# Layer 1's attention: results normalised and turned per unit, weights and token tiles split ahead inside the unit loop

## The reference, cut to what matters

```python
def rms_norm(x, g):
    xf = x.astype(jnp.float32)
    y = xf * lax.rsqrt(jnp.mean(xf * xf, axis=-1, keepdims=True) + EPS)
    return (y * g.astype(jnp.float32)).astype(x.dtype)

# blocked_diff_attention, for every block of 128 queries
s = jnp.einsum('bqphd,bsphd->bphqs', qblk, k, preferred_element_type=jnp.float32) * scale
pr = jax.nn.softmax(s, axis=-1)
w = (pr[:, 0] - lam * pr[:, 1]).astype(v.dtype)
return jnp.einsum('bhqs,bshe->bqhe', w, v)

# diff_mixer, latent tokens
q, k, v = jnp.split(h @ p['w_in'], 3, axis=-1)
q = rms_norm(q.reshape(B, L, 2, C_HEADS, HEAD_DIM), p['q_gain'])
k = rms_norm(k.reshape(B, L, 2, C_HEADS, HEAD_DIM), p['k_gain'])
...
o = blocked_diff_attention(q, kk, vv, lam)
o = rms_norm(o, p['subln']) * (1.0 - p['lam_init'])
return o.reshape(B, L, C_HEADS * 2 * HEAD_DIM) @ p['w_out'], state
```

## Time and profile before

| | us |
|---|---|
| median of 3 runs | 3526.24 (3525.89 to 3528.17) |
| the profiled execution, its own time | 3528.04 |
| its span in the trace | 3525.4 |
| layer 1's attention in it | about 862 (1686 to 2548) |
| PE busy over the span | 3219.6 (91%) |
| DVE busy | 2253.0 (64%) |
| ACT busy | 1852.7 (53%) |

### The profile page before, as it was taken

One profiled execution on the slowest core, in us unless ns is written; L12 is line 12 of the kernel. 1 busy time (PEld: TensorE's weight loads), 2 busy tenths in 40 slices (PEclk: granted clock), 3 DMA queues, 4 the chain that ended last, 5 costly groups with the idle time before them and its releaser, 6 DMA issues. The chain is left out here.

```text
span 3525.4 us, 54805 instructions
## 1 busy us (share of the span) xinstructions
PE 3219.6 (91%) x19994; PEld 2440.7 (69%) x19994; DVE 2253.0 (64%) x2853; ACT 1852.7 (53%) x2549; POOL 559.1 (16%) x319
## 2 busy tenths in 40 slices
PE   6988989997999999997898998989997899999997
PEld 3447777784667667675687887878885567767665
DVE  3557666644666666665686785867746566666665
ACT  2444647522565666664365473654722556666663
POOL 1001010000322333221101101010000233322220
PEclk9989999996999999998899999999997999999998
DMA  7230000228888888885010100100035588888883
GB/s 242 83 104 21 1 21 1 73 102 319 310 304 291 289 301 288 292 292 159 21 40 7 40 7 2 40 7 22 29 116 226 204 299 296 289 291 293 286 303 115
DMA packets 218313, 566.37 MB, mean 161 GB/s; under 512 B 37845, under 2 KB 75418, under 8 KB 217882
## 3 DMA queue, kind: packets, MB, share of 16 engines
q1 hardware_dynamic: 207760, 530.26, 41.9%
q0 software_dynamic: 9472, 33.57, 4.0%
q10 hardware_dynamic: 906, 0.23, 0.0%
HBM read 525.05 MB, written 38.94 MB: 160 GB/s over the span
## 5 line engine op out<-in xcount | busy, mean ns | idle before, releaser
L2342 DVE TENSOR_TENSOR moe_lo<-moe_raw,moeg_hi 128x2048 fp32r<-128x2048 f32 x384 | 884.6, 2339 | 319.8 <-PE psum L2162 154.9
L2244 ACT CAST moeg_hi<-moe_raw 128x2048 fp32r<-128x2048 f32 x384 | 728.9, 1911 | 426.2 <-PE psum L2180 298.0
L933 PE MATMUL psum<-attn_w_hi,attn_hs 128*128 128x256 f32 (+2 forms) x1440 | 382.8, 350 | 54.5 <-DVE attn_w_lo L1281 27.9
L1397 DVE TENSOR_REDUCE attn_neg_max<-psum 128x1 f32<-128x1280 f32 (+1 forms) x216 | 292.5, 1356 | 79.9 <-PE psum L1038 77.7
L933 PEld LDWEIGHTS psum<-attn_w_hi,attn_hs 128*128 128x128 f32 x1440 | 261.1, 195 | 87.3 <-DVE attn_hs L1275 41.7
L1197 ACT ACTIVATE attn_e<-psum,attn_neg_max 128x1280 f32<-128x1280 f32 (+1 forms) x216 | 265.1, 1227 | 79.3 <-DVE attn_neg_max L1397 61.0
L1038 PE MATMUL psum<-attn_ks,attn_qst 128*128 128x512 f32 (+2 forms) x1200 | 283.0, 369 | 16.3 <-ACT attn_qst L1135 6.5
L1135 ACT COPY attn_pt<-psum 128x512 f32<-128x512 f32 (+2 forms) x400 | 192.7, 508 | 153.4 <-PE psum L1051 139.4
L2180 PE MATMUL psum<-moeg_hi,moeh_x_hi 128*128 128x512 f32 x960 | 265.3, 398 | 4.8 <-issue 4.8
L2180 PE MATMUL psum<-moe_lo,moeh_x_hi 128*128 128x512 f32 x960 | 262.5, 395 | 0.0
L2180 PE MATMUL psum<-moeg_hi,moeh_x_lo 128*128 128x512 f32 x960 | 261.1, 393 | 0.0
(11 more groups left out here) (293 smaller groups left out, 5296.4 us busy)
## 6 DMA issues: line engine op xcount, KB each, us to landing
moe_raw<-in_l_w_gate SPq DMA_DIRECT2D x256, 512.0 KB, 3.9
moe_raw<-in_l_w_up SPq DMA_DIRECT2D x256, 512.0 KB, 5.1
moe_raw<-in_l_w_down SPq DMA_DIRECT2D x128, 1024.0 KB, 6.2
ada_w<-in_l_ada_w SPq DMA_DIRECT2D x32, 1024.0 KB, 14.3
lru_ada<-in_l_ada_w SPq DMA_DIRECT2D x16, 1024.0 KB, 7.4
out_w<-in_l_w_out SPq DMA_DIRECT2D x16, 512.0 KB, 5.5
h_rows<-mix_xs SPq DMA_DIRECT2D x16, 512.0 KB, 2.6
attnw_w<-in_l_w_in SPq DMA_DIRECT2D x16, 512.0 KB, 6.7
```

Of the source, the lines that this page charges most:

```text
L933: last = pe.matmul(out, hs[t % 2][:, part, k, :], right, start=(k == 0 and n == 0), stop=(k == KB - 1 and n == 2))
L1397: dve.tensor_reduce(neg_max[:, n:n + 1], m.psum[:, score_at(n):score_at(n) + hi - lo], AX.X, ALU.max, negate=True).then_inc(s["maxed"], 1)
L2244: act.copy(mm.hi[slot % 4][:, :, :], mm.raw[slot][:, :, :]).then_inc(s["hi_ready"], 1)
L2342: dve.tensor_tensor(mm.lo[slot][:, :, :], mm.raw[slot][:, :, :], mm.hi[slot % 4][:, :, :].bitcast(F32), ALU.subtract).then_inc(s["lo_ready ...
```

## The change

It touches `attention` for layer 1 (layer 0's order and sizes stay as they are):

- The results live in five small tiles (`OUT_TILES`) of 128 by 128 in turn, laid over the split keys `khl`, instead of one big `o`. DVE waits at the start of a group until the last results were turned before it writes the keys there.
- POOL makes mean and power of every unit by itself (two instructions of one column, 18 times per group). ACT multiplies the unit's result by it (`normalise`) at the end of the step in which it was squared.
- PE turns the result of unit `u - 3` into the third quarter of the bank in which part 1 of unit `u`'s probabilities stands; ACT copies it to `cat` with the gain (`read_out`) ahead of that part. So 13 results (units 0 to 12) are turned in the loop, and five are left for `turn_out`, in two banks.
- Where `o` was, only `hs[1]` lies (`hs_space`). ACT casts tile 1 of the next group at the end of a group, ahead of the last two `normalise`; in the first group, ahead of the loop.
- ACT and DVE split token tile 0 of the next group at step 12, and the weights at steps 15 to 19, in the order 2, 0, 4, 1, 7, 3, 5, 6, as the probability tiles beneath come free. PE takes tile 0's blocks in that order.
- `norm_mean` and `norm_out` are gone from DVE.

```diff
-    o = put("o", [P, NT, 4 * HD])
+    put("hs_space", [P, NT, 4 * HD])
+    OUT_TILES, OUT_LAG = 5, 3
...
+    khl_at = put.pos[0]
...
-    TURNS = turns_k + 2 * NT + 3 * (units - per_tile) + per_tile + (0, 6)[l]
+    TURNS = turns_k + 2 * NT + 3 * (units - per_tile) + per_tile + (0, 2)[l]
...
+    if l == 1:
+        o = [m.tensor(f"attn1_o{i}", [P, dv], F32, khl_at + i * dv * 4) for i in range(OUT_TILES)]
+    TOKENS = -1
+    ahead_at = [{27 + i: [i - 1] for i in range(KB + 1)},
+                {12: [TOKENS], 15: [2], 16: [0, 4], 17: [1, 7], 18: [3], 19: [5, 6]}][l]
+    w_order = [k for u in sorted(ahead_at) for k in ahead_at[u] if k != TOKENS]
...
@@ program, end of a step @@
-            if l == 0 and not last and units - AHEAD <= u < units:
-                make["ahead"](u - (units - AHEAD))
+            if not last:
+                for piece in ahead_at.get(u, ()):
+                    make["ahead"](piece)
...
+    osum, orstd = ratio[:, 2 * NT:4 * NT], red[:, nz:nz + 2 * NT]
+    out_with = lambda u: u - OUT_LAG if l == 1 and u >= OUT_LAG and u // per_tile < LT else None
+    last_outs = [u for u in range(units) if u > units - per_tile - 1 - OUT_LAG]
+    out_blocks = [[u for u in last_outs if u % 2 == p] for p in range(2)]
@@ gpsimd @@
-                    for i, (lo, hi) in enumerate(NORM_PARTS):
-                        wait_value(m, pool, s["o_mean"], j * 2 + (i + 1))
...
+                    for u in range(units):
+                        wait_value(m, pool, s["o_squared"], j * units + (u + 1))
+                        pool.tensor_scalar(osum[:, u:u + 1], osum[:, u:u + 1], 1.0 / dv, EPS, ALU.mult, ALU.add)
+                        pool.drain()
+                        pool.tensor_tensor(orstd[:, u:u + 1], osum[:, u:u + 1], m.neg_half[:, 0:1], ALU.pow
+                                           ).then_inc(s["o_rstd"], 1)
@@ tensor @@
-                for k in range(KB):
+                for i, k in enumerate(w_order if t == 0 else range(KB)):
                     if t == 0 and lo == 0:
-                        pe.wait_ge(s["w_split"], j * KB + (k + 1))
+                        pe.wait_ge(s["w_split"], j * KB + (i + 1))
...
+                        if part == 1 and out_with(u) is not None:
+                            pe.wait_ge(s["o_normed"], j * units + (out_with(u) + 1))
+                            last = pe.transpose(m.psum[:, at + 2 * P:at + 3 * P], o[out_with(u) % OUT_TILES][:, :], m.ident[:, :])
                         last.then_inc(s["turned"], 1)
...
                 def turn_out():
...
+                    pe.wait_ge(s["o_normed"], j * units + units)
+                    for block in out_blocks:
+                        at = next_turn()
+                        for i, u in enumerate(block):
+                            last = pe.transpose(m.psum[:, at + i * P:at + (i + 1) * P], o[u % OUT_TILES][:, :], m.ident[:, :])
+                        last.then_inc(s["turned"], 1)
@@ scalar @@
                 def project(t):
-                    split_tokens(j, t + 1)
+                    if l == 0 or t >= 1:
+                        split_tokens(j, t + 1)
...
+                        if part == 1 and out_with(u) is not None:
+                            read_out(out_with(u))
...
                         square_out(u - 2)
+                    if l == 1 and part == 1 and u >= 2:
+                        normalise(u - 2)
...
+                def read_out(u):
+
+                    act.wait_ge(s["turned"], j * TURNS + (turn[0] + 1))
+                    at = turn_bank(used[0]) + 2 * P
+                    out = cat[:, ds(j * 2 + u % 2, 1), (u // 2) * P:(u // 2 + 1) * P].rearrange("p o t -> p (o t)")
+                    act.activation(out, m.psum[:, at:at + P], ACT.Copy, scale=m.subln[:, 0:1])
+
+                def normalise(u):
+                    act.wait_ge(s["o_rstd"], j * units + (u + 1))
+                    act.activation(o[u % OUT_TILES][:, :], o[u % OUT_TILES][:, :], ACT.Copy, scale=orstd[:, u:u + 1]
+                                   ).then_inc(s["o_normed"], 1)
...
-                def ahead(i):
-                    if i == 0:
+                def ahead(piece):
+                    if piece == TOKENS:
                         split_tokens(j + 1, 0)
-                    else:
-                        split_weights(j + 1, [i - 1])
+                        return
+                    values_done = {7: units - 2, 5: units - 1, 6: units} if l == 1 else {}
+                    if piece in values_done:
+                        act.wait_ge(s["pv_done"], j * units + values_done[piece])
+                    split_weight(j + 1, piece)
...
                 if l == 1:
+                    for u in (units - 2, units - 1):
+                        square_out(u)
                     if not last_group:
-                        split_tokens(j + 1, 0)
-                        split_weights(j + 1, EARLY_W)
-                    square_out(units - 2)
-                    square_out(units - 1)
-                    if not last_group:
-                        act.wait_ge(s["pv_done"], j * nvalues + nvalues)
-                        split_weights(j + 1, LATE_W)
+                        split_tokens(j + 1, 1)
+                    for u in (units - 2, units - 1):
+                        normalise(u)
                     turn_out()
@@ vector @@
                     dve.wait_ge(s["cache_loaded"], j * (32 * PT_TILES) + 32 * PT_TILES)
+                    if l == 1:
+                        dve.wait_ge(s["turned"], j * TURNS)
...
+                    if not last_group:
+                        for piece in ahead_at.get(u, ()):
+                            if piece == TOKENS:
+                                split_tokens(j + 1, 0)
+                            else:
+                                split_weights(j + 1, [piece])
                 dve.drain()
-                if l == 1:
-                    if not last_group:
-                        split_tokens(j + 1, 0)
-                        split_weights(j + 1, EARLY_W)
-                    norm_mean(1)
-                    if not last_group:
-                        split_weights(j + 1, LATE_W)
-                    norm_out(1)
-                    dve.drain()
```

More of the change, by code:

```diff
@@ L1466, in group @@
                         maxima(u + 1, 1)
-                    if l == 1 and u == units - 1:
-                        norm_mean(0)
-                    if l == 1 and u == units + 1:
-                        norm_out(0)
                     if l == 1 and u % 2 == 0 and u // 2 + 2 < NT:
```

68 lines of the change are left out of this document (18 added, 50 removed).

## The result

The changed kernel takes 3493.62 us (median of 4 runs, 3490.60 to 3494.95), the kernel before 3527.11 (3525.89 to 3528.17): a ratio of 0.9904, 95% interval 0.9887 to 0.9921. The forecast was 3493.

A forecast was written before the change was run, and what follows sets the result against it. PE was taken as the bound, standing still at group borders and hardly stopping in the units. Borders and end -46.5 - 3.0, units and step 12 +10.6 + 6.2, sum -32.7 us: forecast 3493, range 3477 to 3515.

The forecast's parts named there:

- the late last values: End of a group: weight casts and subtractions make unit 17's probabilities be read about 0.4 us later, charged at each border.
- The borders: Between groups: 114.6 us for three borders fall to 23.5, 23.5 and 21.1, together 68.1, a gain of 46.5.
- PE's branch: Ahead of tile 1 at the first two borders: PE's return to the loop's start, formerly hidden, taken as 2.4 us each.
- the margin of 0.9 for block 6: Border, tile 0: the last weight block is subtracted about 4 us behind the last values, and PE asks 4.9 behind.
- The pair of steps: In the units: a pair pays 0.25 for ACT's normalisation and 0.13 for PE's transpose, 0.38; 10.6 us in all.
- Rival B: In the units: ACT's additions are paid in most steps, needing waits and address registers; 17 less gain, 3510 us; chance 0.15.
- Step 12: Token tile 0's split there makes DVE's next maximum start 2.05 us late; three groups cost 6.2 us.
- The end of the stage: From the last values to the last copy: 8.5 us come to 5 to 6, a gain of 3.
- POOL's chain of 0.9 to 1.9: Per unit: POOL's mean and power with hand-overs, called covered by 2.1 us and another 1.1 of ACT's spare.
- The rule weighed: Port shared by DVE and POOL: whichever starts first blocks the other; trace agrees for POOL as loser, not for DVE.
- C: In 56 steps DVE loses the port to POOL, up to 0.85 us per unit, 48 in all: 3541 us; chance 0.03.
- D: In 56 steps POOL is blocked behind DVE and ACT waits: +67, net +34 us, 3560 us; chance 0.04.

The follow-up runs named there:

- e4: The changed kernel with token tile 0 and all weights split behind step 19 instead of ahead: 3498.06 us, ratio 0.9916.
- e8: The changed kernel with the normalisation one step later (six result tensors, not five) and DVE's token tile 0 subtraction at the end of step 14: 3474.48 us.
- e3: The kernel before with only token tile 0 and the weights split ahead, at steps 12 and 15 to 19; results turned at the border: 3515.19 us.
- e6: The changed kernel with token tile 1 of the next group split behind the turned copies again, as before: 3505.41 us, ratio 0.9944.
- e2: The changed kernel with ACT's normalisation one step later and a sixth result tensor in place of five: 3479.96 us, ratio 0.9864.
- e1: The changed kernel with DVE's subtraction for token tile 0 at the end of step 14 instead of step 12: 3489.39 us, ratio 0.9896.
- e5: The changed kernel with one more four-column POOL power, its result unused, ahead of each unit's mean: 3514.06 us, ratio 0.9956.

## Why the prediction was right, and where it wasn't

The mechanism was right: the two waits at each border went, and the units and step 12 paid for it about as forecast. One term failed, the late last values, and the time came so near because errors cancelled.

- *The borders.* 23.5, 23.5 and 21.1 were forecast, 68.1 together; 22.6, 23.7 and 21.7 came, 68.0. Inside, the terms differ and cancel. PE's branch is 1.39 and 1.52, not 2.4, but in e4 and e8 it was 2.07 and 1.72. Tile 0 is 8.9 at the first border, not 8.5: the margin of 0.9 for block 6 was nearer to nothing, and the wait didn't return in full. At the other two it is 10.2, at a clock of 0.64 for its first 4.7 us, which no term had. That the sum of the borders came out to 0.1 us is luck. e3, e4 and e6 show that all three parts are needed for it.
- *The pair of steps.* +0.38 forecast, +0.39 measured, and e2 splits it as forecast (0.27 for ACT's 0.25, and 0.12 left for PE's 0.13). Per group it came to 2.0 to 2.2, not the 2.65 of seven full pairs. The prediction read 0.79 and 0.43 as the idle stretches of all even steps; the kernel before has 0.43 in nearly every pair, and 0.79 once in a looped group, at step 12. The pair that ends there took 13.24 already, so it grew by only 0.03. The rest of ACT's work was hidden as argued: ACT's wait ahead of the turned tiles on odd steps fell from 1.11 to 0.65. Rival B's registers do exist, 0.23 of issue ahead of each looped `read_out` (9.1 us in all), and vanish in ACT's waits for the maximum and for the turned tiles.
- *Step 12.* 2.05 forecast, 1.9 measured (15.16 less 13.27), and e1 and e8 showed its cause. Without a normalisation between exponential and cast (e3) it is 1.4. The third group lost 1.4 more to the clock behind it, which the sum didn't have.
- *The end of the stage.* 3.0 forecast, 2.6 measured.
- *The last values 0.4 late: mis-sized.* They are 1.4 late in each of three groups. The step that failed is the one that let the weight casts alone set this term and called POOL's chain of 0.9 to 1.9 "covered". The chain is 1.5, inside those bounds, and covered in the wide steps, where `read_out`, a copy and a 1.33 us exponential stand before the normalisation. In the last narrow steps there is nothing to cover it, and ACT waits 1.44. The cover was looked up for one kind of step and used for all. But the wait costs only together with the casts. From PE's start on step 14's probabilities to the end of the last values, in the first group, it took 17.61 before, 18.00 with the weights ahead alone (e3: the 0.4 of the forecast), 17.88 with the turning alone (e4), 19.25 with both, and 18.32 with both in e2's order. So 0.93 of the lateness belongs to neither part: ACT waits for POOL, then makes two weight casts of 1.55 together, and only then copies the last probabilities. In the fourth group, which has no casts, ACT waits 1.19 and PE's wait for the last values is 0.43 as before. Of the 14.9 us that ACT stood for `attn_red`, the 1.44 in each of three groups are the costly ones.
- *The rule weighed.* POOL waited for DVE and not the other way: a one-column power took 1.08 beside a DVE subtraction and 0.55 alone, while DVE's maxima kept 1488 ns under e5's 72 extra powers. Those maxima read PSUM. For DVE operations with two SBUF inputs e5 has better cases: here POOL's power began first, DVE's second weight subtraction 0.08 later (two rows in one, the second from 1903.10), and each took its usual time.

```profile
1903.02 1.03 POOL L931 TENSOR_TENSOR rstd<-ones,neg_half 128x4 f32<-128x4 f32 x1 [3.11 <-ACT attn_zc L1254]
1902.24 1.81 DVE L1314 TENSOR_TENSOR attn_w_lo<-attnw_w,attn_w_hi 128x768 fp32r<-128x768 f32 x2
```

In the changed kernel 20 of the 36 subtractions for the split queries began while POOL was at work; they took 0.425 on average, the other 16 took 0.426. Rivals C and D fell with it. The Trainium skill, page "SBUF — State Buffer", section "SBUF: two separate sides", has whichever engine starts first hold the port pair while the other is blocked, a DVE operation with two SBUF inputs among them. These traces agree for POOL as the loser (in the changed kernel a mean begun under a DVE subtraction ended 0.05 after it, having taken 0.52 and once 1.22 in place of 0.19) and disagree for DVE, which lost no time where POOL had started first. The measurement decides.

Sum by term: borders +46.6, end +2.6, units -19.8 (2.1 in four groups, 1.9 and 1.4 in three, 1.4 of clock once, rounded), which is 29.4. (The second way of cutting gives the borders 46.4, and 0.2 to the first two projections.) The time came out nearer than its sum: 32.7 was 3.3 too much, and the time outside the stage was lower by chance or for a reason that isn't known. That 3493 was met to 0.6 us is luck in this part.

Not settled: why the clock fell in the third group and at two borders; why the time outside the stage moves by up to 11 us between kernels with the same code there. The part ahead with own memory for the token tiles, but with results turned at the border, wasn't tried.

## What to carry to other kernels

When work goes to another engine and comes back, check the round trip in every kind of step of the loop, the narrow ones first, because what hides it in a wide step isn't there, and check it together with whatever else the change puts into those steps: each of the two parts alone left the last values nearly on time. One more buffer and one more step of distance gave 13.7 us here; by the stage's parts some 7 of them are the pairs of steps, 2.8 the last values and 1.4 the clock. When work is pulled ahead of a border, choose the step by what waits for it there, not merely somewhere before the border: the same splits were worth 5.8 us in one order and 13.2 in another. And cut a stage into parts whose lengths add up before the experiments, since what moved outside it was up to a third of the stage's gain (7.2 beside 21.9 in e4).

## What the runs showed of the hardware

- The return to the loop's start costs each engine its own time, seen as idle without a releaser: PE 1.39 to 2.07 us ahead of tile 1 in six kernels (2.65 and 2.79 in e5, for a reason that isn't known), ACT 2.05 and 2.22 with a table load of 1.28 behind it in the changed kernel. At the third border, without a branch, PE has no such stretch. PE's was invisible before, under the wait for tile 1.
- The clock differs behind the same idle stretch: behind the 2.99 us in e6 tile 1's first matmul took 0.50 at one border and 0.79 at the next.
- POOL's four-column power in e5, 1.01 us alone, took 1.35 where it ran beside DVE's weight subtractions; its one-column mean took 0.19 alone and 0.52 beside one in the changed kernel. DVE's weight subtraction took its usual 0.95 where POOL had started 0.08 before it (e5).
